# Pool products one gate later, the second GLU after six taps, earlier table loads, reordered splits and filler products in a two-layer encoder step

## What is computed

```python
h = rmsnorm(x, norm_mix)
qa, ka, va, ub, cq, ckv, kpe, ud, gate_in = split_cols(h @ w_in)
ud = ud[..., :512] * sigmoid(ud[..., 512:])                 # GLU, four tiles of 128 channels
o_b = pool_mix(ub, ...)                                     # four groups, windows 2, 4, 8, 16, each @ w_pool[g]
o_d = silu(layernorm(depthwise_conv31(ud)))                 # 31 taps
merged = sum(gates[b] * (o[b] @ w_o[b]) for b in range(4))
x = x + merged @ w_out
x = x + (silu(rmsnorm(x) @ w_ff_gate) * (rmsnorm(x) @ w_ff_up)) @ w_ff_down
```

## Time and profile before

| | |
|---|---|
| median of three runs | 2376.43 us (2376.19 to 2378.64) |
| the profiled execution | 2380.27 us, its span 2378.5 us |
| TensorE busy | 2271.5 us, 96% of the span |
| VectorE, ScalarE, GpSimd busy | 1316.6, 863.2 and 970.1 us |
| mean granted TensorE clock | 0.981 |
| share of the chain that ended last | PE 84%, DVE 11%, ACT 2%, issue 2% |

### The profile page before, as it was taken

The page is one execution under the profiler, slowest core; times in us unless marked ns, Lnnn a source line. Parts: engine busy times, 40 slices in busy tenths (PEclk is TensorE's granted clock), DMA queues, the critical chain, the costliest instruction groups (busy, mean ns, idle before and its releaser), DMA issues.

```text
span 2378.5 us, 39615 instructions
## 1 busy us (share of the span) xinstructions
PE 2271.5 (96%) x14968; PEld 2183.2 (92%) x14968; DVE 1316.6 (55%) x2350; ACT 863.2 (36%) x1684; POOL 970.1 (41%) x988
## 2 busy tenths in 40 slices
PE   6999999999999999999989999999999989999996
PEld 6999898888999999999989989988889989999996
DVE  7995444333337835727599765433332387275364
ACT  3015233444314534525421153334441245254352
POOL 4554354232564342333445444533326623333231
PEclk8999999999999999999999999999999989999998
DMA  5252122011222222222233411211113312222221
GB/s 177 80 182 79 36 72 67 27 41 41 85 101 80 72 89 72 91 70 85 63 130 138 126 52 54 71 50 41 41 32 106 113 52 91 70 89 89 72 80 54
DMA packets 70565, 187.84 MB, mean 79 GB/s; under 512 B 19825, under 2 KB 22481, under 8 KB 69393
## 3 DMA queue, kind: packets, MB, share of 16 engines
q1 hardware_dynamic: 62608, 165.64, 21.5%
q10 hardware_dynamic: 7808, 20.16, 2.5%
HBM read 173.47 MB, written 14.14 MB: 79 GB/s over the span
## 4 chain that ended last, share of the span: by engine, by line
PE 84%; DVE 11%; ACT 2%; issue 2%; DMA 0%; ACTq 0%; SPq 0%; DVEq 0%
PE gemm L681 41%; PE gemm L1143 17%; PE gemm L1133 14%; PE side L1143 3%; DVE rstd L1715 2%; PE side L1016 2%; PE side L996 1%; DVE act_lo L2168 1%; PE side L1003 1%; DVE side L1832 1%; PE side L947 1%; DVE prod L1762 1%; PE side L780 1%; PE side L867 1%; DVE prod L1922 1%
## 5 line engine op out<-in xcount | busy, mean ns | idle before, releaser
L661 POOL TENSOR_TENSOR ring_lo<-w_raw,ring_hi 128x512 fp32r<-128x512 f32 x232 | 308.1, 1330 | 588.9 <-ACT ring_hi L1574 588.8
L642 POOL CAST w_hi<-w_raw 128x384 fp32r<-128x384 f32 x376 | 218.3, 581 | 754.0 <-PE gemm L681 719.5
L644 POOL TENSOR_TENSOR w_lo<-w_raw,w_hi 128x384 fp32r<-128x384 f32 x376 | 447.8, 1191 | 30.1
L681 PE MATMUL gemm<-h_hi,w_hi 128*128 128x320 f32 x1664 | 420.8, 334 | 15.8 <-DVE conv_sample L1795 6.0
L681 PE MATMUL gemm<-h_lo,w_hi 128*128 128x320 f32 x1664 | 382.4, 311 | 0.0
L681 PE MATMUL gemm<-h_hi,w_lo 128*128 128x320 f32 x1664 | 382.4, 311 | 0.0
L681 PEld LDWEIGHTS gemm<-h_hi,w_hi 128*128 128x128 f32 x1664 | 285.8, 191 | 48.2 <-issue 21.6
L1143 PE MATMUL gemm<-act_hi,ring_hi 128*128 128x320 f32 x960 | 300.0, 313 | 18.8 <-issue 9.9
L1143 PE MATMUL gemm<-act_lo,ring_hi 128*128 128x320 f32 x960 | 299.2, 312 | 0.0
L1143 PE MATMUL gemm<-act_hi,ring_lo 128*128 128x320 f32 x960 | 299.2, 312 | 0.0
L681 PEld LDWEIGHTS gemm<-h_lo,w_hi 128*128 128x128 f32 x1664 | 281.6, 190 | 0.0
(11 more groups left out here) (296 smaller groups left out, 4265.3 us busy)
## 6 DMA issues: line engine op xcount, KB each, us to landing
w_raw<-in_ws_ff SPq DMA_DIRECT2D x120, 512.0 KB, 3.3
w_raw<-in_ws_gate SPq DMA_DIRECT2D x64, 512.0 KB, 3.3
w_raw<-in_ws_in SPq DMA_DIRECT2D x44, 512.0 KB, 3.3
w_raw<-in_ws_proj SPq DMA_DIRECT2D x64, 256.0 KB, 2.6
w_raw<-in_ws_out SPq DMA_DIRECT2D x16, 512.0 KB, 3.2
w_raw<-in_ws_fd SPq DMA_DIRECT2D x16, 384.0 KB, 3.0
x_park<-x ACTq DMA_DIRECT2D x2, 2560.0 KB, 12.4
x<-x_park ACTq DMA_DIRECT2D x4, 1280.0 KB, 6.0
```

The lines of the kernel that those rows point to most:

```text
L642: eng.tensor_copy(w_hi[s][:, cols], w_raw[s][:, cols]).then_inc(w_high.sem, 1)
L644: eng.tensor_tensor(w_lo[s][:, cols], w_raw[s][:, cols], w_hi[s][:, cols].bitcast(F32), ALU.subtract).then_inc(w_split.sem, 1)
L661: eng.tensor_tensor(lo, src, hi.bitcast(F32), ALU.subtract).then_inc(lo_plain.sem, 1)
L681: mm = eng.matmul(dst[:, hf, 0:HALF], w, r[k][:, cols] if r in (xu_hi, xu_lo) else r[:, k, cols], start=first and k == 0 and part == 0, st ...
```

## The change

It does these things, in both layers unless said otherwise:

- `pool(2)` on TensorE stands behind gate 5 instead of gate 4, and `pool(3)` behind the first six tiles of gate 6; ACT's list follows.
- On DVE `glu(1)` stands behind 6 instructions of the convolution instead of 24, and the next piece has 30; four of the five memsets move from before `glu(0)` to before `glu(2)`. `first_out(0)` moves behind the first `t2`.
- ACT runs a one-column square root into an unread tile ahead of the norms (`sqrt_table`), which moves the load of the square root's table to there.
- In the first quad DVE does `up_out(1)` and the first two `act_low` and one `sum_low` before the block A12, and so ACT's rounding of A12 comes later.
- `busy(n)` multiplies `ones` by `ones` (fp32, 128x128) n times into a PSUM bank that nobody reads: 12 at the very start and 2 before each of seven tiles of unit 0 (layer 0 alone), 10 before the last merge, and 12, 9 and 5 in the first quad.

```diff
+            def busy(n, bank=7):
+                for _ in range(n):
+                    eng.matmul(B[bank][:, 0:P], ones[:, :], ones[:, :], start=True, stop=True)
+
+            busy(12, 6)
@@ products of unit 0
                         if u == 0:
+                            if l == 0 and k:
+                                busy(2, 6)
                             eng.wait_ge(xu_ready.sem, xu_ready.at(l, k + 1))
@@ TensorE, first gates
                 first_gate(4)
+                first_gate(5)
                 pool(2)
-                first_gate(5)
+                first_gate(6, 0, 6)
                 pool(3)
-                first_gate(6)
+                first_gate(6, 6, KT)
@@ TensorE, before the last merge
+                busy(10)
                 merge_tiles(3 * KT, 8, 12)
@@ TensorE, quad
+                    if q == 0:
+                        busy(12)
                     block_product(n, QX, act(A11), True)
@@
                     eng.wait_ge(p_copy.sem, p_copy.at(l, 5 * q + 3))
+                    if q == 0:
+                        busy(9)
                     block_product(n + 4, QV, act(S1), False)
+                    if q == 0:
+                        busy(5)
                     block_product(n + 5, QZ, act(A22), False)
@@ ACT
+            def sqrt_table():
+                eng.activation(unused[:, :], eps[:, :], ACT.Sqrt)
+
                 square_x(0, -1, k)
+            sqrt_table()
@@
                 first_gate(4)
+                first_gate(5)
                 pool(2)
-                first_gate(5)
                 pool(3)
                 first_gate(6)
@@ DVE
-                first_out(0, sg)
                 for k in range(KT):
@@
+                    if k == 0:
+                        first_out(0, sg)
@@
-                    last = min(done + 24, 2 * TAPS * (i + 1)) if i < 3 else 8 * TAPS
+                    last = done + (6, 30, 24)[i] if i < 3 else 8 * TAPS
                     conv(done, last)
                     done = last
+                    if i == 1:
+                        eng.memset(pbp[:, :, 0:PH], 0.0).then_inc(hist_zeroed.sem, 1)
...
@@ DVE, first quad
-                act_block(af[A12], 4, lo_half)
-                act_sum(af[S4][:, :, :], af[A12][:, :, :], af[S2][:, :, :], ALU.subtract, 19)
+                up_out(1)
                 act_low(A11)
                 act_low(S3)
-                up_out(1)
                 sum_low(FF_QUADS[0] + 1)
+                act_block(af[A12], 4, lo_half)
                 sum_low(FF_QUADS[0] + 2)
+                act_sum(af[S4][:, :, :], af[A12][:, :, :], af[S2][:, :, :], ALU.subtract, 19)
```

More of the change, by code:

```diff
@@ L236, in encoder @@
         eps, at = sb("eps", [P, 1], F32, at)
+        unused, at = sb("unused", [P, 1], F32, at)
         sg, at = sb("gate", [P, T], F32, at)
@@ L1774, in _ @@
                 eng.memset(cvp[:, :, 0:CH], 0.0).then_inc(hist_zeroed.sem, 1)
[L1775 to L1778, removed]
                 def glu(i):
@@ L1842, in _ @@
                     glu(i)
-                    last = min(done + 24, 2 * TAPS * (i + 1)) if i < 3 else 8 * TAPS
+                    last = done + (6, 30, 24)[i] if i < 3 else 8 * TAPS
                     conv(done, last)
                     done = last
+                    if i == 1:
+                        eng.memset(pbp[:, :, 0:PH], 0.0).then_inc(hist_zeroed.sem, 1)
+                        eng.memset(ntk[:, :, :], 0.0).then_inc(pads.sem, 1)
+                        eng.memset(kT[64:128, 0, :], 0.0).then_inc(pads.sem, 1)
+                        eng.memset(kT[0:64, 1, :], 0.0).then_inc(pads.sem, 1)
                 for u in range(8, 12):
```

## The result

The changed kernel takes 2351.88 us (2351.35 to 2352.74, four runs), where the kernel before takes 2377.53 beside it: a ratio of 0.9893, with the interval 0.9875 to 0.991. The forecast was 2348.0 with a range of 2340 to 2358. The profiled execution took 2352.74, its span 2351.0 against 2378.5 before. That is 27.5 less where the sum said 28.65; on the medians it is 25.7, since the profiled execution of the kernel before, 2380.27, was 2.7 above its median and that of the changed kernel 0.9. One execution of the kernel before (7856.95 us) and one of the kernel with the second GLU alone (8062.68 us) took over three times as long as the others and count in no ratio.

The account below looks back on a forecast made before the run. TensorE, busy 2271.5 of 2378.5 us, was taken as the bound, each wait costing itself plus the slow-clock stretch behind it. Terms summed to -28.65: 2351.6 from the profiled execution, 2347.8 on the median; forecast 2348.0, range 2340 to 2358.

Parts of the forecast that it names:

- two pool terms: Pool products: waits and the slow stretches behind them gone, 6.4 us less in layer 0 and 7.05 in layer 1.
- Second GLU: Second conv gate: DVE reaches `glu(1)` 7.9 us sooner, ending the waits and slow stretches in both layers, -10.9 us.
- what is late next is the third GLU: Second conv gate: after the second GLU the third is the next possible delay, with some two us of cover.
- no wait of 1.4 us or more: Sign that the forecast is right: no TensorE wait that long remains in the second conv gate's stage.
- Ten fillers: Before the last merge: 2.2 us of fillers fit free in a 2.66 us wait and hold the clock, -3.4 us.
- Start of layer 0: Table load gone, product of sums faster, `first_out(0)` out of the way, against fillers: -1.4 us, between -2.7 and +1.1.
- Norms: Table load leaves the path: -0.5 us at layer 1's norm, 0 at the feed-forward norm, -1.25 at the last.
- First quad: Block n 1.7 us sooner, new wait of about 6 before n+2, fillers running on: +1.1 a layer, +2.2 both.
- Case C: Rival, first quad: not delayed, ACT's copy in time because DVE's five low parts are shorter; 2341 us, chance 0.10.
- B: Rival, merge and start: the fillers don't hold the clock, so their gain is lost; 2354 us, chance 0.14.
- D: Rival: the wait moves on to the third GLU or `pool(3)`, with a slow stretch; +9, 2357 us, chance 0.12.
- E: Rival, all 98 fillers: they run on the path at half clock, 0.44 us each; 2391 us, chance 0.03.

Follow-up runs that it names:

- e1_pool_only: The kernel before with only the two pool products moved later among the gates, on TensorE and in ACT's list: 2364.58 us, ratio 0.9943.
- e2: The kernel before with only the second GLU behind six convolution taps and four memsets moved later: 2369.61 us, ratio 0.9967.
- e8_issues_later: The changed kernel with ACT's eight DMA issues of the sample bias moved behind its sigmoid of the second gate: 2349.28 us, ratio 0.9878.
- e3: The kernel before with only ten products of ones added before the last merge of each layer: 2377.39 us, ratio 0.9997.
- e4_tables_only: The kernel before with only the one-column square roots ahead of the norms, first_out left in place: 2375.05 us, ratio 0.999.
- e7: The changed kernel with DVE's old order ahead of the first quad and all fillers kept: 2348.59 us, ratio 0.9874.
- e6: The changed kernel without the nine and the five products of ones inside the first quad: 2347.87 us, ratio 0.9876.

## Why the prediction was right, point by point

The total came out 27.5 and 28.9 us less by the spans of the two profiles, where the sum said 28.65. That it came so close is in part luck: the second GLU brought some 2.5 us less than its term, and the two quads and the start of layer 0 together 2.5 more.

- **The bound and the price of a wait.** Right, and shown by `e1_pool_only`: itself and the slow stretch behind it. The two pool terms came out within 0.05 us.
- **Second GLU.** The mechanism was right, the size was not: -10.9 predicted, -8.2 to -8.4 in both profiles of the changed kernel and in `e2`. The step that failed is "what is late next is the third GLU". That one was in time; what was late next was ACT's sigmoid of the same pair, behind its DMA issues, 1.12 and 1.37 us. In layer 1 the wait of 1.45 on ACT in the earlier trace rows was exactly this one, and I counted it as gone with DVE's. With the issues moved as well, `e8_issues_later`, the term is there in full, -11.3. The sign "no wait of 1.4 us or more" held by a hair in the first profile (1.37) and not in the second (1.51).
- **Ten fillers.** Right: free in the wait, and the clock held each time. The 0.22 us from the rows was the right price from start to start; the whole row of ten products, twenty records, took 2.50 us. The estimate by the Trainium skill ("TensorE: Matmul & The Clock Gate", Back-to-back issue gap), 0.056 for one, did not hold here. Their worth was over-estimated, 1.3 instead of 1.7, because the clock doesn't fall every time without them, and the time of `e3` doesn't show even that.
- **Start of layer 0.** Not resolved. The changed kernel's first profile, -1.95, is inside the bounds of -2.7 and +1.1, its second, -2.96, is beyond them: -1.95 to -3.81 among profiles of the changed start with its fillers, -1.26 and -1.95 without them, -3.87 with the tables alone, 0 to -1.61 with the old start. What the fillers do here is open. The first twelve took 5.49 us, 0.46 each, and fill the 6.0 us for which TensorE waits there for the first weights in the kernel before.
- **Norms.** Right in size: -1.22 and -1.37 for the last, where -1.25 was forecast, less only where its product of sums ran at the low clock; about nothing for the feed-forward part. There the reason given was only part of it, since `e4_tables_only` keeps the old order and gains 0.22 of 1.28 as well. The second part of a table switch, 1.38 us by the Trainium skill ("ScalarE: Activation LUTs", What ACT_TABLE_LOAD costs), showed in none of these waits. The -0.28 and -0.60 at the start of layer 1 can't be told from the -0.25 to -0.38 of kernels with the old start.
- **First quad.** Block n started 1.7 us sooner as worked out, and the new wait ahead of block n+2 came, 5.4 for "about 6", and the fillers ran on past their wait. The term, +1.1, measured -0.16 to +1.12 over six passes, 0.4 on average (changed, twice, and `e8`). The step that failed is that DVE's list, being the same instructions in another order, delivers for block n+4 as late as before, at about 787.3. Case C's reason was true: the five low parts took 7.10, not 9.26 (why is left open under `e7`). That made the operands ready 2 us sooner, and the nine fillers ate it. `e6` shows the price of the nine and five, 1.8 us a layer.
- **Rivals.** B didn't happen: no low clock behind the merge's fillers. D happened in another place, at about a third of its size in a layer. E was true of 14 of the 36 fillers of a layer, and those took 0.22 each from start to start, not 0.44. C's gain was there to be had, but not in this kernel.

## What to carry to other kernels

Where one engine is busy all the time and a short wait is followed by a low clock, price the wait from the granted clock of the stretch behind it too; here 3.9 us cost 6.4 to 7. Fillers can pay only in a wait that ends later than they do and that has no other cure; where an edit shortens the wait, the same fillers become the wait. Before moving a producer forward, look at every engine that has to deliver for the same consumer, and at the DMA issues in its list, since a row's releaser may be only the last semaphore and not what was in the way.

## What the runs showed of the hardware

An idle time of 2.66 us, the same to the last digit, was followed by a low clock in eight of ten passes and by a full one in two, without any difference in code at that place. So one profile can't say that such a wait costs its slow stretch; the pool products' 3.9 us did so in each of the passes seen here (before, `e2`, `e3` and `e4`, in both layers).

DVE's subtractions of 128x1280 elements took 1.48 us, but two of five took 2.58 and 2.55 in eleven of the twelve passes with the old order of the quad, while POOL's `ring_lo` ran beside them. In the twelfth, layer 0 of `e7`, they stayed at 1.48, and POOL's two took 6.89 together where they took 1.34 and 1.53 in layer 1. So the same instructions in another order can take longer or shorter, here by 2.2 us.
